# Output stage of an expert layer: one pass over V, with three token tiles resident in PSUM and three summed through two shared banks

## What is computed

```python
def expert_block(args):
    hx, ix, gx = args
    act = jax.nn.gelu(jnp.einsum('tkd,td->tk', u_tab[ix], hx))
    return jnp.einsum('tk,tkd->td', gx * act, v_tab[ix])
...
x = x + g2 * peer(h, *peer_w)      # and then the final RMSNorm, times its weight lnf
```

## Time and profile before

| what | value |
|---|---|
| median of three runs | 3805.85 us |
| profiled execution, its own time | 3806.96 us |
| its span | 3805.2 us |
| output stage within the span | about 2566.5 to 3805.2 us |
| PE busy over the span | 3415.7 us (90%) |
| VectorE busy over the span | 2887.7 us (76%) |
| HBM traffic over the span | 807.65 MB read, 138.11 MB written |

### The profile page before, as it was taken

The page is one execution under the profiler, slowest core; times in us unless marked ns, Lnnn a source line. Parts: engine busy times, 40 slices in busy tenths (PEclk is TensorE's granted clock), DMA queues, the critical chain, the costliest instruction groups (busy, mean ns, idle before and its releaser), DMA issues. The chain is left out here.

```text
span 3805.2 us, 52216 instructions
## 1 busy us (share of the span) xinstructions
PE 3415.7 (90%) x17854; PEld 2993.1 (79%) x17854; DVE 2887.7 (76%) x4884; ACT 1418.4 (37%) x2552; POOL 1770.8 (47%) x1003
## 2 busy tenths in 40 slices
PE   5999969697999999999889899997997998989998
PEld 2998859444999999899888888996776776767776
DVE  4544247595578899998999999657886888878886
ACT  2321135243222222224777777523332333333332
POOL 0000012110211778786888888765554654555510
PEclk8979989798999999999999999998998999999999
DMA  5225334542112778776989888879999999989976
GB/s 197 74 84 180 114 105 144 167 143 80 34 34 66 233 247 257 242 262 230 341 331 348 329 342 334 329 271 356 361 384 358 354 357 353 363 327 375 371 270 210
DMA packets 416593, 947.30 MB, mean 249 GB/s; under 512 B 38035, under 2 KB 230211, under 8 KB 413267
## 3 DMA queue, kind: packets, MB, share of 16 engines
q1 hardware_dynamic: 293252, 457.63, 35.9%
q0 software_dynamic: 114480, 417.47, 29.9%
q10 hardware_dynamic: 8736, 70.78, 4.8%
HBM read 807.65 MB, written 138.11 MB: 249 GB/s over the span
## 5 line engine op out<-in xcount | busy, mean ns | idle before, releaser
L1872 POOL DMA_INDIRECT hT<-peer_v,hT x336 | 595.6, 1773 | 487.3 <-DVE hrow L1884 408.1
L1725 PE MATMUL ps<-h_hi,u_hi 128*128 128x384 f32 x2048 | 699.0, 341 | 31.0 <-POOL u_lo L1611 23.2
L1725 PE MATMUL ps<-h_lo,u_hi 128*128 128x384 f32 x2048 | 689.0, 336 | 0.0
L1725 PE MATMUL ps<-h_hi,u_lo 128*128 128x384 f32 x2048 | 689.0, 336 | 0.0
L1962 PE MATMUL ps<-v_hi,a_hi 128*128 128x512 f32 x1512 | 487.2, 404 | 125.8 <-DVE ga_rest L1896 114.9
L1962 PE MATMUL ps<-vw_rest,a_hi 128*128 128x512 f32 x1512 | 476.4, 397 | 0.0
L1962 PE MATMUL ps<-v_hi,ga_rest 128*128 128x512 f32 x1512 | 474.6, 396 | 0.0
L1962 PEld LDWEIGHTS ps<-v_hi,a_hi 128*128 128x128 f32 x1512 | 283.3, 193 | 219.6 <-DVE vw_rest L1894 147.0
L1842 ACT ACTIVATE v_hi<-vw 128x1024 fp32r<-128x1024 f32 x256 | 270.6, 1057 | 410.9 <-DMA vw<-peer_v 399.1
L1607 POOL DMA_INDIRECT hT<-u_rows,hT x224 | 376.0, 1679 | 95.8 <-issue 51.2
L1884 DVE SCALAR_TENSOR_TENSOR hrow<-hT,dots,hrow 128x1024 f32<-128x1024 f32 x336 | 420.4, 1279 | 0.0
(11 more groups left out here) (336 smaller groups left out, 6040.2 us busy)
## 6 DMA issues: line engine op xcount, KB each, us to landing
vw<-peer_v SPq DMA_DIRECT2D x256, 512.0 KB, 8.5
uw<-u_T SPq DMA_DIRECT2D x128, 512.0 KB, 4.3
s_d<-so SPq DMA_DIRECT2D x256, 192.0 KB, 5.0
gates_d<-big ACTq DMA_DIRECT2D x24, 2048.0 KB, 10.0
gt<-gates_d SPq DMA_DIRECT2D x64, 768.0 KB, 8.8
ga<-s_d SPq DMA_DIRECT2D x256, 192.0 KB, 8.8
wmr<-w_modT SPq DMA_DIRECT2D x32, 512.0 KB, 4.0
tok_d<-st SPq DMA_DIRECT2D x45, 256.0 KB, 2.2
```

What stands on the lines that cost most here:

```text
L1725: mm = pe.matmul(g.ps[4 + 2 * s + b][:, 0:HALF], u[s][:, k, :], h[:, k, b * HALF:(b + 1) * HALF], start=(k == 0 and i == 0), stop=(k == KD ...
L1872: pool.indirect_dma_start(rows[n % NU], None, g.v_rows, bass.IndirectOffsetOnAxis(ap=g.pick[m % GT][:, m // GT:m // GT + 1], axis=0)).then ...
```

## The change

Each V block is loaded once. The ring becomes 8 slots, handled as two halves of BL = 4 experts (a block j; NB = 32 blocks). `ga`, `a_hi`, `a_lo` become 768 wide (all six tiles). Tiles 0 to 2 of the dense ones ("kept") stay in banks 0 to 5 to the end. Tiles 3 to 5 ("taken") take turns in banks 6 and 7: for a block of four experts `taken(j, i, t)` forms tile t's sum over these four (12 matmuls per bank), and VectorE's `take(j, t)` adds it to `acc` in SBUF, or copies it there for j = 0. TensorE's order in a `period` is taken 0, kept, taken 1, kept, taken 2, kept, kept, where each `kept` is one expert of the next block for three tiles (18 matmuls). Loads of block j wait until TensorE has ended all taken sums of block j - 2. The rows are spread in 202 steps; `hrow`, `hT` and `gt` are used again for the end.

```diff
-    RING, TA, TB = 4, 3, DENSE - 3
+STEPS = 6 + 7 * 28
+    RING, BL, TP = 8, 4, 3
+    NB, TR = NE // BL, DENSE - TP
...
+            for j in range(2):
+                gates(j, j)
+                loads(j, j)
+            with sp.Fori(1, NB // 2) as m:
+                for i in range(2):
+                    sp.wait_ge(a_ready, m * (2 * BL) + BL * (i - 1))
+                    gates(m * 2 + i, i)
+                    sp.wait_ge(bank_done, m * (4 * TR) + 2 * TR * (i - 1))
+                    loads(m * 2 + i, i)
...
+            def take(j, t):
+                for q in range(2):
+                    dve.wait_ge(bank_done, 2 * (TR * j + t) + q + 1)
+                    part = acc[:, t, q * 512:(q + 1) * 512]
+                    if j == 0:
+                        z = dve.tensor_copy(part, g.ps[6 + q][:])
+                    else:
+                        dve.wait_ge(bank_read, 2 * (TR * (j - 1) + t) + q + 3)
+                        z = dve.tensor_tensor(part, part, g.ps[6 + q][:], ALU.add)
+                    z.then_inc(bank_read, 1)
...
+            for e in range(BL + 2):
+                gated(e)
+                step = rows_between(step)
+            for j in range(NB - 2):
+                for t in range(TR):
+                    take(j, t)
+                    if j == NB - 3:
+                        finish_first(t)
+                    step = rows_between(step)
+                    for e in ((BL * (j + 1) + 2 + t,) if t < 2 else (BL * (j + 2), BL * (j + 2) + 1)):
+                        gated(e)
+                        step = rows_between(step)
...
+            def kept(j, i, k, first=False):
+                pe.wait_ge(v_lo_ready, j * BL + (k + 1))
+                pe.wait_ge(a_lo_ready, j * BL + (k + 1))
+                for t in range(TP):
+                    for q in range(2):
+                        three(g.ps[2 * t + q], i * BL + k, t, q, first, False)
+            def taken(j, i, t):
+                for q in range(2):
+                    pe.wait_ge(bank_read, j * (2 * TR) + (2 * t + q + 1))
+                    for k in range(BL):
+                        mm = three(g.ps[6 + q], i * BL + k, TP + t, q, k == 0, k == BL - 1)
+                    mm.then_inc(bank_done, 1)
...
+            for t in range(TR):
+                taken(NB - 2, 0, t)
+            for t in range(TP):
+                last_kept(t)
+                taken(NB - 1, 1, t)
```

More of the change, by code:

```diff
@@ L1794, in outputs @@
-        rows = [g.hT[:, i, 0:D] for i in range(NU)]
[L1795 to L1800, removed]
+        a, a_lo = zip(*(twin(nc, ctx, f"ga{i}", [P, TE]) for i in range(RING)))
@@ new lines, in outputs @@
+        v_loaded, a_loaded, row_loaded, g_loaded = psem("vl"), psem("al"), g.ou_rows, psem("gl", 2)
+        v_hi_ready, v_lo_ready, a_ready, a_hi_ready, a_lo_ready = (sem(n) for n in ("vhi", "vlo", "a", "ahi", "alo"))
+        bank_done, bank_read, tile_done = sem("bank"), sem("read"), sem("tile")
+        added, g2_in, first_in, dense_in, late_in, first_done = (sem(n) for n in ("added", "g2", "xq", "xd", "late", "qdone"))
+        ms_ready, root_done, chain, fin, stored = (sem(n) for n in ("ms", "root", "chain", "fin", "st"))
@@ L1801, in outputs @@
         ctx.callback(clear_sems, nc, sems)
         block = ctx.enter_context(nc.Block())
-        span = lambda p: (0, TA * P) if p == 0 else (TA * P, TE)
-        bank = lambda p, t: 2 * ((p * TA + t) % 4)
+        tile_rows = lambda t: g.x1_d[t * P:(t + 1) * P, :]
         @block.sync
         def _(sp):
[L1808 to L1820, removed]
-                    sp.dma_start(vw[s][:], g.peer_v[:, one, :].rearrange("p o d -> p (o d)")).then_inc(v_loaded[s], 16)
[L1822 to L1833, removed]
@@ L1837, in _ @@
         def _(act):
[L1838 to L1853, removed]
@@ new lines, in root @@
+            def root(i):
+                act.wait_ge(ms_ready, i + 1)
+                act.activation(ss[:, 3 * i:3 * i + 3], ss[:, 3 * i:3 * i + 3], ACT.Sqrt).then_inc(root_done, 1)
+            with act.Fori(0, NE // RING - 1) as m:
+                for s in range(RING):
+                    ready(m * RING + s, s, m)
+            for s in range(RING - 2):
+                ready(NE - RING + s, s, NE // RING - 1)
+            root(0)
+            for s in range(RING - 2, RING):
+                ready(NE - RING + s, s, NE // RING - 1)
@@ L1866, in _ @@
+            root(1)
+            root(2)
         @block.gpsimd
         def _(pool):
-            for n in range(VA + VB):
+            for n in range(VO):
                 m = V1 + n
@@ L1898, in square @@
[L1898 to L1928, removed]
-                if e in (122, 123, 124):
-                    for c in range(2 * (e - 122), 2 * (e - 121)):
-                        scale(c, (3, 4, 5, 0, 1, 2)[c])
@@ new lines, in finish_kept, with finish_taken @@
+            def finish_kept(t):
+                dve.wait_ge(tile_done, t + 1)
+                for q in range(2):
+                    z = dve.tensor_tensor(yp[t][:, q * 512:(q + 1) * 512], g.ps[2 * t + q][:], g2[:, q * 512:(q + 1) * 512], ALU.mult)
+                own.link(z)
+                finish(FINISH.index(GT + t), GT + t, yp[t])
+            def finish_taken(t):
+                take(NB - 1, t)
+                dve.wait_ge(bank_read, 2 * (TR * (NB - 1) + t) + 4)
+                y = acc[:, t]
+                own.link(dve.tensor_tensor(y, y, g2[:], ALU.mult))
+                finish(FINISH.index(GT + TP + t), GT + TP + t, y)
@@ new lines, in scale @@
+            def scale(i):
+                dve.wait_ge(root_done, i + 1)
+                own.link(dve.reciprocal(ss[:, 3 * i:3 * i + 3], ss[:, 3 * i:3 * i + 3]))
+                for c in range(3 * i, 3 * i + 3):
+                    t = FINISH[c]
+                    dve.scalar_tensor_tensor(x[t], x[t], ss[:, c:c + 1], lnf, ALU.mult, ALU.mult).then_inc(fin, 1)
+            step = 0
+            for e in range(BL + 2):
[10 more added lines that the diff above has]
+                        step = rows_between(step)
@@ new lines, in _ @@
+            dve.sem_inc(ms_ready, 1)
+            for t in range(TR):
+                take(NB - 2, t)
+                if t < 2:
+                    gated(NE - 2 + t)
+            dve.wait_ge(late_in, 48)
+            scale(0)
+            dve.wait_ge(dense_in, 16 * (NT - 2 - GT))
+            finish_kept(0)
+            finish_taken(0)
+            finish_kept(1)
+            dve.sem_inc(ms_ready, 1)
+            finish_taken(1)
+            scale(1)
+            finish_kept(2)
+            finish_taken(2)
@@ L1947, in _ @@
+            dve.sem_inc(ms_ready, 1)
+            scale(2)
         @block.tensor
         def _(pe):
-            pe.sem_inc(o_done, RING)
-            def products(p, e, first=False, last=False):
-                for s in range(RING):
-                    pe.wait_ge(v_lo_ready, p * NE + e + (s + 1))
-                    pe.wait_ge(a_lo_ready, p * NE + e + (s + 1))
-                    begin, end = first and s == 0, last and s == RING - 1
-                    for t in range(TA if p == 0 else TB):
-                        rows_ = slice(t * P, (t + 1) * P)
-                        if p == 1 and begin and t:
-                            pe.wait_ge(ya_done, 2 * t)
-                        for i, (aa, v) in enumerate(((a_hi, v_hi), (a_hi, v_lo), (a_lo, v_hi))):
-                            for q in range(2):
-                                mm = pe.matmul(g.ps[bank(p, t) + q][:], aa[s][:, rows_], v[s][:, q * 512:(q + 1) * 512],
-                                               start=(begin and i == 0), stop=(end and i == 2), skip_group_check=True)
-                    mm.then_inc(o_done, 1)
@@ L1976, in _, with three @@
-            for p in range(2):
-                products(p, 0, True)
-                with pe.Fori(1, NE // RING - 1) as j:
-                    products(p, j * RING)
-                if p == 0:
-                    products(p, NE - RING, last=True)
-            last_blocks()
+            pe.sem_inc(bank_read, 2)
+            def three(bank, s, t, q, start, stop):
+                for i, (aa, v) in enumerate(((a_hi, v_hi), (a_hi, v_lo), (a_lo, v_hi))):
+                    mm = pe.matmul(bank[:], aa[s][:, t * P:(t + 1) * P], v[s][:, q * 512:(q + 1) * 512],
+                                   start=(start and i == 0), stop=(stop and i == 2), skip_group_check=True)
+                return mm
@@ new lines, in period, with last_kept @@
+            def period(j, i):
+                taken(j, i, 0)
+                kept(j + 1, 1 - i, 0)
+                taken(j, i, 1)
+                kept(j + 1, 1 - i, 1)
+                taken(j, i, 2)
+                kept(j + 1, 1 - i, 2)
+                kept(j + 1, 1 - i, 3)
+            def last_kept(t):
+                pe.wait_ge(v_lo_ready, NE)
+                pe.wait_ge(a_lo_ready, NE)
+                for q in range(2):
+                    for k in range(BL):
```

(12 more changed lines are left out.)

108 lines of the change are left out of this document (57 added, 51 removed).

## The result

The changed kernel takes 3722.75 us, the median of four runs (3714.26 to 3735.81), against 3809.82 for the kernel before: a ratio of 0.9769, with a 95% interval of 0.9748 to 0.9789. It is faster by 87 us where 143 were forecast; the forecast's 3663 us is 60 us under the median. The profiled execution took 3714.26 us, with a span of 3712.6.

What follows compares the result with a forecast made beforehand. Waits from the ring of slots were taken to cost TensorE 169 us. Forecast: 2577.3 (first matmul before) + 1046 (TensorE's floor) + 18 (start) + 6 (scatter) + 15.0 (end) = 3662.3 us span, hence 3663 us; range 3647 to 3730.

Steps and rivals of the forecast that it cites:

- the 6 for scatter: In the steady periods: 0.2 us a period over 30 periods for varying load landings, 6 us in all.
- the forecast's own case: Whole stage bound by TensorE, load landings mostly hidden: 3645 to 3690 us, chance 0.65.
- rival 1: Landing of each block's loads sets the period: 53 to 100 us more, about 3735 us; chance 0.18.
- the new wait: TensorE waits for `take(j-1, 0)`, behind two gatings and rows on VectorE; hidden while L is under 7.1 us.
- the queue is empty at A: When `taken(j-2, 2)` ends and block j's loads issue, earlier loads are through, so only row gathers compete.
- The start: Stage start: TensorE waits before `taken(0, 1)` for experts 4 and 5 to land; 18 us lost, bounds 10 to 25.
- L: Time from the end of `taken(j-2, 2)`, when block j's loads issue, to its first gate multiply; forecast 6.7 us.
- The upper bound: Longest landing time of a block's first loads, from loaded transfers in the earlier profile: 10.1 us.
- a price (2.9 us): TensorE after a long idle: matmuls run at half speed (1.2 GHz) for a while, 2.9 us lost.
- VectorE as the bound: VectorE's takes and small waits give 33 to 34 us a period: about 30 us more, 3695 us; chance 0.08.
- Slower than before: All loads wait for one moment; each period idles past 3 us, restarts at half speed: about 3900 us; chance 0.06.
- No gain for lack of memory rate: Rows and V share a full memory path, so the period stays at 38 us: 3800 us; chance 0.03.

Runs made afterwards that it cites:

- Run 1: The changed kernel with each row gather fetching 128 columns (64 KB) instead of 1024 (512 KB), VectorE's work unchanged: 3649.25 us, ratio 0.9575 to the kernel before.
- run 7: The reordered kernel with one more copy of its bank into a spare tile before each take half: 3662.04 us, ratio 0.9584 to the kernel before.
- runs 9 and 10: Next block's gates issued before a block's first `ga`, in the changed kernel and the reordered one: 3965.7 and 3950.75 us, ratios 1.0407 and 1.0373 to the kernel before.
- run 3: The changed kernel reordered on VectorE: one, two, one experts gated behind the three takes instead of one, one, two; 3658.13 us, ratio 0.9598 to the kernel before.
- runs 11 and 12: The reordered kernel (one, two, one experts gated behind the takes) and the changed kernel, both repeated unaltered on one chip: 3658.03 and 3719.36 us.

## Why the forecast missed by 56 us

The forecast gain was 143 us, the measured one 87; in time, 3663 against 3722.75. In the span of the profiled execution, with 55.6 us in place of the 6 for scatter, the sum gives 3711.9, and 3712.6 was measured. The rest of the 60 us is that the median lies 8.5 us above the profiled execution, where the forecast had put it 1.1 below.

The time lies inside the stated range of 3647 to 3730, but that is not to the mechanism's credit: the forecast's own case, a stage bound by TensorE, was put at 3645 to 3690. The upper end had been drawn to 3730 to take in half of rival 1, and rival 1 is what came. Its signs came too: 327 GB/s where over 340 were foreseen, and TensorE waiting on a `take` in the blocks in which VectorE had waited 4.1 to 7.3 us for `ga`.

**Right.** The floor: 32.64 us a period, 0.2267 a matmul with three in a row into one bank. The clock, wherever nothing waits. The cost of `gated` (the 768-wide instructions took 0.95 us, 0.87 start to start) and of `take` (0.68 a half, 0.60 start to start where the second follows at once). VectorE's sum: 29.6 forecast, 29.2 measured. The place of the new wait and, in the mean, its limit; that the queue is empty at A. The end: 15.0.

**Right by luck.** The start: 20 us lost against an unhindered stage where 18 were taken. The prediction had the landing of experts 4 and 5 end this wait. In the trace the first matmul was 12 us later than thought (2594.4 instead of 2582.6), the experts after it came without any wait, and VectorE, never idle from the first gate multiply at 2591.3 to the first take at 2619.3, set the time by its own work.

**Wrong: one term.** "L = 6.7, excess mostly 0; for scatter I take 0.2 us a period over 30 periods, 6 us." L was 6.0 to 10.2 us, 8.0 in the mean, and the loss 55.6 us, 2.0 a period. The step behind it that failed: "rows alone compete, two or three of them in flight: 1 us". In the bad block at 2881 four gathers were issued around the burst, and the row queue took half of the DMA engines' time just then. The upper bound that I had worked out from the earlier trace rows, 10.1 us, was what came in the worst blocks. I priced that case as rival 1 at 53 us and more, and gave it 0.18. Run 1, in which only the rows' bytes changed, shows the cause: L was 4.9 to 6.1 us and the loss was gone.

**A term left out.** Beyond the wait, some late blocks pay for the clock. In the changed kernel TensorE waited 36.2 us for `acc` in the stage; the loss is 55.6, so 19 us are slow matmuls and smaller effects. Eight of the 16 blocks over 7.1 us restarted with 7 to 12 matmuls 0.43 us apart, which cost 1.6 us in seven of them and 2.7 in block 9, 14 us in all; another 0.3 us beyond the wait is lost in every late block. The length of the idle time does not tell which: 1.8 us was followed by the half clock in block 23, 3.3 us was not in block 26. I had a price (2.9 us) but not in the forecast.

**Rivals.** VectorE as the bound: refuted (runs 1, 7). Slower than before: not here, but its mechanism exists, and runs 9 and 10 show it: at L of 16 to 20 us the one-pass kernel is 4% slower than two passes. No gain for lack of memory rate: refuted, 349 GB/s were moved in run 3.

**Open.** Why some gathers keep GpSimd for 4.62 us and others for 0.94 or 1.75 was not settled. In the changed kernel nine blocks have such a gather about 6 us before the issue and three more behind it within 2 us of the issue, and these nine have L from 8.0 to 10.2 us. But seven blocks are late without one; and in run 3 gathers of 4.62 us begin 3.4 or 2.2 us before the issue, the next one only 1.5 us or more after it, and L there is 5.2 to 6.3 us. No run moved these gathers by themselves. Whether the evenly paced rows of the reordered kernel keep L low by themselves, apart from the limit, was not tested.

## What to carry to other kernels

When a buffer is freed in blocks, find what stands behind the first wait for its refill on each in-order engine, work out the longest landing that this order hides, and compare it with the loaded landing time in the trace, not with that of a quiet queue. Raising that limit by reordering, or freeing slots one at a time, cost nothing here; the reorder gave 61 us beyond the 87 of the change (runs 11 and 12). A limit worked out from mean row counts hides that blocks differ by a row. A late landing can be paid twice, once as the wait and once more where TensorE restarts at half its clock.

## What the runs showed of the hardware that I had not expected

- Behind a gates transfer of 3072 pieces of 512 bytes, SyncE's next issue took 9.43 us at the stage's start, and 13.18 for the next such, against 0.33 for the V issue of a later block (2815.34).
- Eight row gathers, begun together with that first gates transfer, went with a first gate multiply 23 us after the first V issue; 13.5 with gates in 12 KB pieces, 12.7 with the gathers held, 14.8 with narrow ones.
- VectorE was busy for 99.96% of 700 us in run 7, beside a TensorE that never idled there, and it cost TensorE nothing measurable.
- TensorE restarted at half its clock after 8 of the 16 late blocks' waits, and not in the order of their length: after 1.8 us in blocks 15 and 23, not after 3.3 us in block 26.
